# First norm's tables made by TensorE, router logits interleaved with output products, two filler products

## The chip, the cores and the metric

The kernel runs on one core of one Trainium2 chip. The metric is device time in microseconds, from the start to the end of one execution. A core has TensorE (PE in the profile, with its weight loads listed apart as PEld), VectorE (DVE), ScalarE (ACT), GpSimd (POOL) and SyncE (SP, which here issues most of the DMAs), and 16 DMA engines that move data between HBM and the core's SBUF.

## The reference, cut to what matters

384 frames (256 of a new stream, 8 times 16 of running ones) of width 1024 pass one encoder layer. Everything is float32.

```python
m = W_out(concat[beta_ret * Retention(x), beta_conv * ShortConv(x)])   # the mixer
h = LayerNorm1(alpha * x + m)              # gain ln1_g, offset ln1_b
logits = h @ w_router + b_router           # 32 experts, top 4 of 32, softmax over the 4
gate, up = h[tok] @ w_gu[e] + b_gu[e]      # w_gu: 32 x 1024 x 2048, 8 MB an expert
f += g * (((clip(up) + 1) * min(gate) * sigmoid(1.702 * gate)) @ w_down[e] + b_down[e])   # 4 MB an expert
y = LayerNorm2(alpha * h + f)
```

## The kernel before

The program has two parts. The **mixer** projects the input, runs retention and convolution, and multiplies by `w_out`. The **expert part** takes the experts two at a time (a pair), all 32 in turn, and then up to 24 overflow blocks for experts with more than 64 tokens. Each pair needs 24 pieces of weights of 1 MB (128 x 2048 floats): 8 of `w_gu` for each expert, 4 of `w_down` for each expert.

**Rooms.** Pieces land in SBUF in 12 rooms of `ring` and, once the mixer's data are dead, in 4 or 5 of `old_rooms`. Pair 0 uses six side rooms too: `EARLY` (pieces 6 and 7, in `early_rooms`) and `LATE` (pieces 16 to 19, in `over_q`, the last old room, `in_lnp` and `in_xy`). `in_lnp` is the tile `lnp`, 2 x 1024 floats on each partition. Every DMA of weights is issued by SP in the order of the program. SP issues one when the semaphore `piece_used`, which TensorE counts up as it finishes each piece, says that the room is free. So a wait at the head of SP's program holds every transfer behind it.

**Between the mixer and pair 0.** TensorE runs, in program order: the output products (`wout(t, c)`, three float32r products of 512 columns for each of 8 chunks; `t` is one of three tiles of 128 frames, and this is the second half of the output columns), the transposes of the unnormalized rows (`transpose_h(t, n)`, half a row each), the router products (`logits(t, n)`, 32 columns), the ranks of tokens within experts (`early_ranks`, `ranks`), the first products of pair 0's accumulation with the biases (`gate_up_bias(0)`), and the gather of pair 0's tokens (`gather_first`, products with the one-hot `onehot`). VectorE adds the residual and takes row statistics (`residual(t, n)`, which raises `h_raw`; `row_stats`), then picks experts (`choose(t)`, which raises `mask_ready`). In VectorE's program `residual(2, 1)` and `row_stats(2, 3)` stand between `choose(0)` and `choose(1)`. ScalarE copies the transposes and normalizes rows.

**The first norm's gain and offset** are applied to `hid` for all later pairs by VectorE in `gain_and_offset`: three multiplications and three additions of 1024 columns, with both vectors lying in `lnp`, spread over all partitions by two DMAs that ScalarE's queue issues at the end of the mixer. Only after that (`h_ready`) may SP load piece 18 (`LATE[2]`) into `in_lnp`. Pair 0 itself takes gain and offset by column from the small table `ln1_t`. `pair(None)` is pair 0 on TensorE: `gate_up(0)`, `gates`, `count`, `gate_up(1)`, `down(0)`, `down(1)`, and then `gather()` for pair 1.

**Early in the mixer** the semaphore `o_free` tells TensorE that VectorE has read the retention's banks; VectorE raises it before `gate_rows(0)`.

Of the kernel before, what the change touches and what calls it, by code (L numbers as in the profile page):

```python
# [29 lines left out]
ALU = mybir.AluOpType  # L30
# [99 lines left out]
def build(nc, x_tok, x_t, s_ret, conv_in, w_in, w_out, chan, beta_ret, ln1, ln2, w_router, b_router,  # L130
# [3 lines left out]
    with es:  # L134
# [143 lines left out]
        chan_in, bias_in, ln1_in, ln2_in, router_in = map(sem, ("chan_in", "bias_in", "ln1_in", "ln2_in", "router_in"))  # L278
# [13 lines left out]
        gn_var, gn_rstd, o_free, o_ready_m = map(sem, ("gn_var", "gn_rstd", "o_free", "o_ready_m"))  # L292
# [7 lines left out]
        row_shift, norm_ready, h_ready = map(sem, ("row_shift", "norm_ready", "h_ready"))  # L300
        half_gathered, first_xg, first_xg_v = map(sem, ("half_gathered", "first_xg", "first_xg_v"))
# [111 lines left out]
        def _(sp):  # L413
# [87 lines left out]
            def aside_pieces(pair, ea, eb):  # L501
# [6 lines left out]
                for j, units in cycled[:ahead] + aside + cycled[ahead:]:  # L508
# [16 lines left out]
                    if pair == 1 and j == 0:  # L525
                        sp.wait_ge(h_ready, NT)
                        first_side(LATE[2])
# [55 lines left out]
            first_side(LATE[3])  # L583
            sp.wait_ge(logit_mm, NT)
# [32 lines left out]
        def _(pe):  # L617
# [125 lines left out]
            def first_streams():  # L743

                pe.wait_ge(vm_ready, 2)
                pe.wait_ge(o_free, NT)
                pe.wait_ge(stp_out, 1)
                streams(0)
                streams(1)
# [124 lines left out]
            for t in range(NT - 1):  # L874
                wout(t, range(4, KC))
            transpose_h(0, 0)
            transpose_h(0, 1)
            wout(NT - 1, (4,))
            logits(0, 0)
            wout(NT - 1, (5,))  # L880
            logits(0, 1)
            transpose_h(1, 0)
            wout(NT - 1, (6,))
            transpose_h(1, 1)
            wout(NT - 1, (7,))
            logits(1, 0)
            transpose_h(2, 0)
# [15 lines left out]


# [176 lines left out]
            def pair(turn, odd=False, last=False):  # L1081
# [14 lines left out]
                if not first:  # L1096
# [4 lines left out]
                        | ({2: count_before, 6: by_expert} if first else {}))  # L1101
# [3 lines left out]
                     | ({2: overflow_tables} if first else {}) | ({6: lambda: sums_so_far(2)} if last else {}))  # L1105
# [35 lines left out]
        def _(act):  # L1141
# [271 lines left out]
        def _(dve):  # L1413
# [106 lines left out]
            for t in range(NT):  # L1520
# [4 lines left out]
                ins.then_inc(o_free, 1)  # L1525
# [418 lines left out]
```

## Time and profile before

| | |
|---|---|
| median of 3 runs (lowest, highest) | 1113.93 us (1113.84, 1114.98) |
| the profiled execution's own time | 1113.32 us |
| its span, first to last instruction | 1111.4 us |
| TensorE busy | 1073.5 us, 97% |
| VectorE, ScalarE, GpSimd busy | 328.0, 207.4, 90.2 us |
| DMA: bytes, mean rate | 436.27 MB, 393 GB/s |
| mean granted TensorE clock | 0.994 of 2.4 GHz |

The chip's profiler recorded one execution. Busy shares are means over parts with different limits. A TensorE that the profile calls busy may still wait between products, since the ends of matmuls are modelled. A float32 matmul appears as two records. A read of the rate of DMA over short stretches tells when all rooms are full and the transfers stand still.

### The profile page before, as it was taken

What the parts mean: (1) busy time and instruction counts of PE and PEld (TensorE: products, weight loads), DVE (VectorE), ACT (ScalarE), POOL (GpSimd) and SP (SyncE); (2) the same over time, 40 slices, a digit from 0 to 9 for tenths busy, and PEclk for the clock granted to TensorE, in tenths of its full rate; (3) what the DMA queues carried; (4) which work ended last, traced back from release to release, by engine and by line L of the source; (5) the groups of instructions that cost most, each with busy time, mean ns of one, the idle gap of its engine ahead of it and who ended that gap; (6) DMA issues with size and microseconds to landing.
All of it is one profiled execution on the core that took longest, in us unless ns stands there. A gap on an engine that the chain in (4) does not pass through costs nothing.

```text
span 1111.4 us, 13640 instructions
## 1 busy us (share of the span) xinstructions
PE 1073.5 (97%) x5552; PEld 544.8 (49%) x5552; DVE 328.0 (30%) x601; ACT 207.4 (19%) x361; POOL 90.2 (8%) x50
## 2 busy tenths in 40 slices
PE   9999999999999999999999999999898989898995
PEld 6889988344434343434343434343434343342532
DVE  3487764512131312121212121212131312112134
ACT  3243333120111120202020202020111111110122
POOL 4675500000000000000000000000000000000002
PEclk9999999999999999999999999999999999999998
DMA  9972589999999999999999999999999999999995
GB/s 351 325 243 76 163 331 404 364 428 407 426 429 425 428 428 428 426 424 430 429 428 429 427 429 428 429 427 428 430 428 427 429 428 428 426 430 428 428 427 204
DMA packets 56611, 436.27 MB, mean 393 GB/s; under 512 B 8128, under 2 KB 18112, under 8 KB 29088
## 3 DMA queue, kind: packets, MB, share of 16 engines
q1 hardware_dynamic: 50048, 428.68, 92.9%
q10 hardware_dynamic: 6528, 7.09, 1.9%
q8 instruction: 26, 0.43, 0.2%
q14 instruction: 9, 0.07, 0.0%
HBM read 431.78 MB, written 3.97 MB: 392 GB/s over the span
## 4 chain that ended last, share of the span: by engine, by line
PE 67%; DMA 25%; DVE 1%; issue 0%; POOL 0%; ACT 0%; POOLq 0%; SPq 0%; DVEq 0%
PE bank L1012 25%; DMA ring<-w_down 25%; PE bank L1044 18%; PE bank L944 8%; PE bank L637 5%; PE bank L1073 1%; PE bank L993 1%; PE bank L864 1%; PE bank L1075 1%; PE bank L854 1%; PE bank L1021 1%; PE bank L800 1%; PE bank L780 1%; PE bank L786 1%; PE bank L803 1%; PE bank L804 1%
## 5 line engine op out<-in xcount | busy, mean ns | idle before, releaser
L1012 PE MATMUL bank<-ring,xg 128*64 128x512 f32 x1536 | 345.3, 595 | 7.2 <-DMA ring<-w_gu 7.1
L1012 PEld LDWEIGHTS bank<-ring,xg 128*64 128x64 f32 x1536 | 105.0, 136 | 209.1 <-issue 188.0
L1044 PE MATMUL bank<-ring,act_t 128*64 128x512 f32 x672 | 151.0, 595 | 8.3 <-DMA ring<-w_down 8.3
L1012 PE MATMUL bank<-old_rooms,xg 128*64 128x512 f32 x496 | 112.3, 595 | 3.7 <-DMA old_rooms<-w_gu 3.7
L1784 DVE SCALAR_TENSOR_TENSOR oo_lo<-oo_raw,gate_s,oo_hi 128x512 fp32r<-128x512 f32 x32 | 24.0, 752 | 311.0 <-ACT oo_hi L1288 311.0
L1820 DVE TENSOR_SCALAR gate_c<-bank 128x512 f32<-128x512 f32 x32 | 22.1, 691 | 249.8 <-PE bank L1012 249.8
L944 PEld LDWEIGHTS bank<-onehot,hid 128*128 128x128 f32 x720 | 85.9, 196 | 12.2 <-issue 12.2
L1044 PEld LDWEIGHTS bank<-ring,act_t 128*64 128x64 f32 x672 | 46.1, 137 | 92.8 <-issue 78.0
L944 PE MATMUL bank<-onehot,hid 128*128 128x128 f32 x720 | 88.8, 283 | 0.0
L1798 DVE TENSOR_TENSOR xy<-xy,bank 128x512 f32<-128x512 f32 x84 | 52.7, 683 | 107.6 <-PE bank L1075 107.6
L1380 POOL TENSOR_TENSOR rstd<-veps,minus_half 128x1 f32<-128x1 f32 x6 | 3.3, 545 | 961.7 <-DVE veps L1580 961.4
L1363 POOL TENSOR_TENSOR w_parts<-ring,w_parts 128x1024 fp32r<-128x1024 f32 x27 | 74.5, 2764 | 52.8 <-ACT w_parts L1159 52.8
L1012 PEld LDWEIGHTS bank<-old_rooms,xg 128*64 128x64 f32 x496 | 34.2, 136 | 66.7 <-issue 57.6
L1315 ACT COPY oo_raw<-bank 64x512 f32<-64x512 f32 x63 | 36.6, 581 | 159.9 <-PE bank L1044 159.1
L1044 PE MATMUL bank<-old_rooms,act_t 128*64 128x512 f32 x256 | 60.0, 609 | 3.8 <-DMA old_rooms<-w_down 3.8
L1299 ACT ACTIVATE sig<-gate_c 128x512 f32<-128x512 f32 x32 | 20.2, 630 | 177.6 <-DVE gate_c L1820 177.6
L1301 ACT COPY act_t<-bank 128x512 f32<-128x512 f32 x32 | 18.8, 586 | 167.0 <-PE bank L993 167.0
L1277 ACT CAST gt<-bank 128x384 fp32r<-128x384 f32 x16 | 7.7, 479 | 201.2 <-PE bank L956 201.2
L637 PE MATMUL bank<-w_parts,x_hi 128*128 128x512 f32 x180 | 44.8, 395 | 0.3 <-ACT w_parts L1159 0.3
L1159 ACT CAST w_parts<-ring 128x1024 fp32r<-128x1024 f32 x27 | 28.4, 1053 | 65.9 <-PE bank L637 60.3
L1073 PE MATMUL bank<-oo_hi,gt 128*128 128x512 f32 x90 | 38.6, 429 | 0.0
L637 PEld LDWEIGHTS bank<-w_parts,x_hi 128*128 128x128 f32 x180 | 33.6, 187 | 9.5 <-issue 1.5
(258 smaller groups left out, 942.9 us busy)
## 6 DMA issues: line engine op xcount, KB each, us to landing
ring<-w_gu SPq DMA_DIRECT2D x90, 2048.0 KB, 30.0
ring<-w_down SPq DMA_DIRECT2D x41, 2048.0 KB, 33.0
old_rooms<-w_gu SPq DMA_DIRECT2D x30, 2048.0 KB, 28.6
old_rooms<-w_down SPq DMA_DIRECT2D x18, 1024.0 KB, 24.8
old_rooms<-w_down SPq DMA_DIRECT2D x7, 2048.0 KB, 30.5
ring<-w_in SPq DMA_DIRECT2D x13, 1024.0 KB, 14.5
ring<-w_gu SPq DMA_DIRECT2D x12, 1024.0 KB, 6.9
over_q<-w_down SPq DMA_DIRECT2D x3, 2048.0 KB, 15.2
```

The lines of the kernel that those rows point to most:

```text
L637: mm = pe.matmul(out, lhs, rhs, start=(n == 0 and c == 0), stop=(n == 2 and c == KC - 1))
L944: mm = pe.matmul(bank[6 + c // 4][:, (c % 4) * 128:(c % 4 + 1) * 128], hid[:, t, :].rearrange("p (q m k) -> p q k m", m=128, k=GU_RUN) [:, ...
L1012: mm = pe.matmul(bank[2 * a + n][64 * hf:64 * hf + 64, :], xg[:, c, 64 * a:64 * a + 64], w[:, col:col + 512], start=False, stop=(c == KC - 1))
L1044: mm = pe.matmul(bank[b][64 * hf:64 * hf + 64, :], act_t[:, a, c % 4, 64 * (c // 4):64 * (c // 4) + 64], w[:, c % run, hf * 512:(hf + 1) * ...
L1073: pe.matmul(bank[comb_banks[i]][:, :], gt[:, t * 128:(t + 1) * 128], oo_hi[:, hf, :], start=True, stop=False)
L1159: act.copy(w_parts[:, n % PARTS, 0, :], w).then_inc(w_hi_ready, 1)
L1299: act.activation(sig[:, :], gate_c[:, :], ACT.Sigmoid, scale=SIG).then_inc(sig_ready, 1)
L1315: act.copy(oo_raw[64 * a:64 * a + 64, hf, :], bank[down_banks[a]][64 * hf:64 * hf + 64, :]).then_inc(out_ready, 1)
L1363: pool.tensor_tensor(w_parts[:, n % PARTS, 1, :], w, w_parts[:, n % PARTS, 0, :].bitcast(F32), ALU.subtract).then_inc(w_lo_ready, 1)
L1784: dve.scalar_tensor_tensor(oo_lo[:, hf, :], oo_raw[:, hf, :], gate_s[:, 0:1], oo_hi[:, hf, :].bitcast(F32), ALU.mult, ALU.subtract).then_i ...
L1798: dve.tensor_tensor(xy[:, t, o], xy[:, t, o], bank[comb_banks[i]][:, :], ALU.add)\
L1820: dve.tensor_scalar(gate_c[:, :], bank[2 * a][:, :], LIMIT, None, ALU.min).then_inc(gate_ready, 1)
```

## The change

1. `lnp` is no longer loaded by DMA for the first norm. TensorE makes gain and offset over all partitions by itself: `ln1_rows(n)`, eight products of a broadcast column of `ln1_t` with the identity (128 columns each), into banks 0 and 1. It does so twice within pair 0: in `gate_up(1)` ahead of chunk 1, and in `down(0)` ahead of chunk 6. VectorE multiplies or adds straight from the banks (`rows_with`).
2. `LATE[2]` needs no wait on `h_ready` now and is issued right after `LATE[3]`, ahead of `EARLY`.
3. The router's products and transposes are spread between output products of tiles 1 and 2; `gate_up_bias(0)` goes behind the last `logits`.
4. Two products of the identity with constants whose output nobody reads, `keep_busy(384)` and `keep_busy(256)`, stand around `logits(2, 0)` and `early_ranks()`.
5. `o_free` is gone; TensorE waits for `o_ready_m`, raised after `gate_rows(0)`.

```diff
@@ SP
-                    if pair == 1 and j == 0:
-                        sp.wait_ge(h_ready, NT)
-                        first_side(LATE[2])
             sp.wait_ge(h_raw, 2 * NT)
             first_side(LATE[3])
+            first_side(LATE[2])
             sp.wait_ge(logit_mm, NT)
@@ PE
             def first_streams():
                 pe.wait_ge(vm_ready, 2)
-                pe.wait_ge(o_free, NT)
+                pe.wait_ge(o_ready_m, 1)
...
+            def keep_busy(columns):
+                pe.matmul(bank[0][:, 0:columns], ident, cst[:, 0:columns], start=True, stop=True)
+            wout(0, range(4, KC))
             transpose_h(0, 0)
+            wout(1, (4, 5))
             transpose_h(0, 1)
-            wout(NT - 1, (4,))
+            wout(1, (6,))
             logits(0, 0)
-            wout(NT - 1, (5,))
+            wout(1, (7,))
             logits(0, 1)
+            wout(2, (4,))
             transpose_h(1, 0)
-            wout(NT - 1, (6,))
+            wout(2, (5,))
             transpose_h(1, 1)
-            wout(NT - 1, (7,))
+            wout(2, (6,))
             logits(1, 0)
+            wout(2, (7,))
+            logits(1, 1)
             transpose_h(2, 0)
-            logits(1, 1)
             transpose_h(2, 1)
+            keep_busy(384)
             logits(2, 0)
+            early_ranks()
+            keep_busy(256)
+            logits(2, 1)
             pe.wait_ge(sel_ready, 1)
             gate_up_bias(0)
-            early_ranks()
-            logits(2, 1)
...
+            def ln1_rows(n):
+                if n == 0:
+                    pe.wait_ge(up_ready, 1)
+                else:
+                    pe.wait_ge(ln1_used, NT)
+                for c in range(KC):
+                    mm = pe.matmul(bank[c // 4][:, (c % 4) * 128:(c % 4 + 1) * 128],
+                                   ln1_t[:, n, c:c + 1].to_broadcast([128, 128]), ident, start=True, stop=True)
+                mm.then_inc(ln1_mm, 1)
...
-                        | ({2: count_before, 6: by_expert} if first else {}))
+                        | ({1: lambda: ln1_rows(0), 2: count_before, 6: by_expert} if first else {}))
...
-                     | ({2: overflow_tables} if first else {}) | ...
+                     | ({2: overflow_tables, 6: lambda: ln1_rows(1)} if first else {}) | ...
@@ ACT
-            act.wait_ge(piece_used, IN_PIECES + 2)
-            for n in range(2):
-                act.dma_start(lnp[:, n, :], ln1[n:n + 1, :].to_broadcast([128, D])).then_inc(ln1_in, 16)
@@ DVE
-                ins.then_inc(o_free, 1)
+            link(ins)
...
-            def gain_and_offset():
-                dve.wait_ge(ln1_in, 32)
-                for t in range(NT):
-                    ins = dve.tensor_tensor(hid[:, t, :], hid[:, t, :], lnp[:, 0, :], ALU.mult)
-                link(ins)
-                for t in range(NT):
-                    dve.tensor_tensor(hid[:, t, :], hid[:, t, :], lnp[:, 1, :], ALU.add).then_inc(h_ready, 1)
+            def rows_with(n, op, done):
+                dve.wait_ge(ln1_mm, n + 1)
+                for t in range(NT):
+                    dve.tensor_tensor(hid[:, t, :].rearrange("p (b n) -> p b n", b=2),
+                                      hid[:, t, :].rearrange("p (b n) -> p b n", b=2), banks[:, 0:2, :], op)\
+                        .then_inc(done, 1)
...
-            gain_and_offset()
...
                             slots_of(p + 1)
+                        if first:
+                            rows_with(0, ALU.mult, ln1_used)
...
                 if first:
                     tables()
+                    dve.wait_ge(ln1_used, NT)
+                    rows_with(1, ALU.add, h_ready)
```

How TensorE's order moves. First, the end of the router: before, from the last output product's follower to the gather (L814 are transposes, L827 logits, L864 the bias products, L840 and L841 ranks, L854 the gather):

```order
L804 MATMUL bank<-out_parts,mixed_lo 128x512
L827 MATMUL bank<-gg,xt 128x32 x4
L814 MATMUL bank<-cst,hid 128x128 x4
L827 MATMUL bank<-gg,xt 128x32 x4
L814 MATMUL bank<-cst,hid 128x128 x4
L827 MATMUL bank<-gg,xt 128x32 x4
L864 MATMUL bank<-biasp,sel 64x512 x4
L841 MATMUL bank<-vv,cst 128x32
L840 MATMUL bank<-vv 128x32
L841 MATMUL bank<-vv,cst 128x32
L827 MATMUL bank<-gg,xt 128x32 x4
L854 MATMUL bank<-onehot,hid 128x128 x13
```

The same place after the change, where every line number is one less and L875 is `keep_busy`, from the last record of `wout(2, 7)` on:

```order
L803 MATMUL bank<-out_parts,mixed_lo 128x512
L826 MATMUL bank<-gg,xt 128x32 x4
L813 MATMUL bank<-cst,hid 128x128 x8
L875 MATMUL bank<-cst 128x384
L826 MATMUL bank<-gg,xt 128x32 x4
L840 MATMUL bank<-vv,cst 128x32
L839 MATMUL bank<-vv 128x32
L840 MATMUL bank<-vv,cst 128x32
L875 MATMUL bank<-cst 128x256
L826 MATMUL bank<-gg,xt 128x32 x4
L863 MATMUL bank<-biasp,sel 64x512 x4
L853 MATMUL bank<-onehot,hid 128x128 x13
```

The bias products went from ahead of the ranks to the end, two fillers came in, and all output products now stand ahead of `logits(1, 1)`.

Second, TensorE in pair 0's second `gate_up`, from the bias products to the transposes of the activations (L1012 are products of `gate_up`, L913 and L914 `count_before`), before:

```order
L864 MATMUL bank<-biasp,sel 64x512 x4
L1012 MATMUL bank<-ring,xg 64x512 x8
L913 MATMUL bank<-vv,cst 96x1
L914 MATMUL bank<-vv 1x1
L1012 MATMUL bank<-ring,xg 64x512 x8
L993 MATMUL bank<-cst,act_h 128x128 x4
```

and after, where L1030 are the products of `gate_up` and L919 is `ln1_rows`:

```order
L863 MATMUL bank<-biasp,sel 64x512 x4
L1030 MATMUL bank<-ring,xg 64x512 x4
L919 MATMUL bank<-cst,ln_t 128x128 x8
L1030 MATMUL bank<-ring,xg 64x512 x4
L931 MATMUL bank<-vv,cst 96x1
L932 MATMUL bank<-vv 1x1
L1030 MATMUL bank<-ring,xg 64x512 x8
```

Eight products came in behind chunk 0, that is ahead of the room-freeing piece 9 and all that follow; eight more stand in `down(0)` ahead of chunk 6.

Third, SP's issues between the mixer and pair 1's weights, before (`xy` is `LATE[3]`, `lnp` is `LATE[2]`, L490 are pieces of pair 1):

```order
L479 DMA ring<-w_gu 128x2048 x7
L483 DMA xy<-w_down 128x2048
L479 DMA early_rooms<-w_gu 128x2048 x2
L483 DMA ring<-w_down 128x2048 x2
L490 DMA ring<-w_gu 128x4096
L483 DMA lnp<-w_down 128x2048
L490 DMA ring<-w_gu 128x4096 x4
```

and after:

```order
L480 DMA ring<-w_gu 128x2048 x7
L484 DMA xy<-w_down 128x2048
L484 DMA lnp<-w_down 128x2048
L480 DMA early_rooms<-w_gu 128x2048 x2
L484 DMA ring<-w_down 128x2048 x2
L491 DMA ring<-w_gu 128x4096 x5
```

`LATE[2]` moved from behind the first piece of pair 1 to the place ahead of `EARLY`.

## Rows read from the trace of the kernel before

**Rows 1.** The page: its span line and the rate in 40 equal slices.

```profile
span 1111.4 us, 13640 instructions
GB/s 351 325 243 76 163 331 404 364 428 407 426 429 425 428 428 428 426 424 430 429 428 429 427 429 428 429 427 428 430 428 427 429 428 428 426 430 428 428 427 204
```

**Rows 2.** Stretches: sum, PE, PEld, DVE, ACT, POOL busy, granted clock, DMA share, GB/s.

```profile
196.00:198.00 2.00, 2.00 (x12) 0.67 (x10) 2.00 (x3) 0.00 (x0) 0.00 (x0) 1.00 0.44 90
...
254.00:258.00 4.00, 4.00 (x21) 1.15 (x17) 0.00 (x0) 0.00 (x0) 0.00 (x0) 1.00 0.88 299
302.00:1092.00 790.00, 766.92 (x3900) 329.10 (x3898) 162.63 (x280) 114.73 (x212) 0.00 (x0) 1.00 1.01 427
```

**Rows 3.** Timeline of SP's DMA issues: start, duration, line, tile.

```profile
195.97 0.33 SPq L483 DMA_DIRECT2D ring<-w_down  x1
...
202.50 0.33 SPq L483 DMA_DIRECT2D lnp<-w_down  x1
...
244.81 0.33 SPq L490 DMA_DIRECT2D ring<-w_gu  x1
...
254.66 0.33 SPq L494 DMA_DIRECT2D ring<-w_down  x1
```

**Rows 4.** The chain that ended last: start, duration, piece.

```profile
251.18 6.87 PE bank L1012 x32
...
305.73 6.87 PE bank L1012 x32
...
640.13 31.91 DMA ring<-w_down
```

**Rows 5.** Timeline of TensorE from the last output product to pair 0.

```profile
179.84 0.39 PE L804 MATMUL bank<-out_parts,mixed_lo 128*128 128x512 f32 x1
...
182.63 0.98 PE L827 MATMUL bank<-gg,xt 128*128 128x32 f32 x8
...
184.38 0.41 PE L841 MATMUL bank<-vv,cst 128*128 128x32 f32 x2 [0.22 <-DVE vv L1649]
...
186.19 4.55 PE L854 MATMUL bank<-onehot,hid 128*128 128x128 f32 x26
...
191.16 2.90 PE L854 MATMUL bank<-onehot,hid 128*128 128x128 f32 x22
193.99 10.52 PE L1012 MATMUL bank<-ring,xg 128*64 128x512 f32 x48
```

**Rows 6.** Timeline of VectorE around the choice of tile 1's experts.

```profile
180.34 0.69 DVE L1598 SCALAR_TENSOR_TENSOR hid<-xy,bank 128x512 f32<-128x512 f32 x1 [0.31 <-PE bank L804]
...
182.36 0.25 DVE L1639 SCALAR_TENSOR_TENSOR vv<-bank,rstd,vv 128x32 f32<-128x32 f32 x1 [0.17 <-PE bank L827]
...
183.95 0.37 DVE L1649 TENSOR_REDUCE vv<-vv 128x32 f32<-128x128 f32 x1
```

**Rows 7.** Stretches of 2 us in which the granted clock fell.

```profile
186.00:188.00 2.00, 2.00 (x10) 2.00 (x11) 1.48 (x10) 1.97 (x5) 0.00 (x0) 0.50 1.03 434
188.00:190.00 2.00, 2.00 (x15) 2.00 (x14) 0.37 (x1) 0.30 (x2) 0.00 (x0) 0.72 1.03 426
...
230.00:232.00 2.00, 2.00 (x6) 0.57 (x8) 0.45 (x3) 0.00 (x0) 0.00 (x0) 0.52 1.00 426
232.00:234.00 2.00, 2.00 (x8) 0.56 (x4) 0.00 (x0) 0.00 (x0) 0.00 (x0) 0.62 1.03 442
```

**Rows 8.** Timeline of TensorE: raw float32 products, the gather for pair 1.

```profile
4.77 5.42 PE L669 MATMUL bank<-ring,hid 128*128 128x512 f32 x12
...
244.70 5.92 PE L944 MATMUL bank<-onehot,hid 128*128 128x128 f32 x48
```

**Rows 9.** Timelines of VectorE and TensorE where `o_free` is waited for.

```profile
115.79 2.22 DVE L1530 TENSOR_TENSOR qo<-qo,gg 128x512 f32<-128x512 f32 x1
117.99 1.15 PE L739 MATMUL bank<-tmp,kk 32*128 32x256 f32 x16
```

**Rows 10.** The page's costliest groups: VectorE's sums from a bank.

```profile
L1798 DVE TENSOR_TENSOR xy<-xy,bank 128x512 f32<-128x512 f32 x84 | 52.7, 683 | 107.6 <-PE bank L1075 107.6
```

More of the change, by code:

```diff
@@ L277, in build @@
         xt_in, x_in, cst_in, mcst_in, st_in = map(sem, ("xt_in", "x_in", "cst_in", "mcst_in", "st_in"))
-        chan_in, bias_in, ln1_in, ln2_in, router_in = map(sem, ("chan_in", "bias_in", "ln1_in", "ln2_in", "router_in"))
+        chan_in, bias_in, ln2_in, router_in = map(sem, ("chan_in", "bias_in", "ln2_in", "router_in"))
         rows_stored, retp_stored = sem("rows_stored"), sem("retp_stored")
@@ L291, in build @@
         chan_mm, c_out, u_out, conv_ready = map(sem, ("chan_mm", "c_out", "u_out", "conv_ready"))
-        gn_var, gn_rstd, o_free, o_ready_m = map(sem, ("gn_var", "gn_rstd", "o_free", "o_ready_m"))
+        gn_var, gn_rstd, o_ready_m = map(sem, ("gn_var", "gn_rstd", "o_ready_m"))
         kd_ready, stp_mm, stp_out = sem("kd_ready"), sem("stp_mm"), sem("stp_out")
@@ L300, in build @@
         row_shift, norm_ready, h_ready = map(sem, ("row_shift", "norm_ready", "h_ready"))
+        ln1_mm, ln1_used = sem("ln1_mm"), sem("ln1_used")
         half_gathered, first_xg, first_xg_v = map(sem, ("half_gathered", "first_xg", "first_xg_v"))
@@ L873, in _ @@
             router_sums()
-            for t in range(NT - 1):
-                wout(t, range(4, KC))
+            def keep_busy(columns):
+                pe.matmul(bank[0][:, 0:columns], ident, cst[:, 0:columns], start=True, stop=True)
+            wout(0, range(4, KC))
             transpose_h(0, 0)
+            wout(1, (4, 5))
             transpose_h(0, 1)
-            wout(NT - 1, (4,))
+            wout(1, (6,))
             logits(0, 0)
-            wout(NT - 1, (5,))
+            wout(1, (7,))
             logits(0, 1)
+            wout(2, (4,))
             transpose_h(1, 0)
-            wout(NT - 1, (6,))
+            wout(2, (5,))
             transpose_h(1, 1)
-            wout(NT - 1, (7,))
+            wout(2, (6,))
             logits(1, 0)
+            wout(2, (7,))
+            logits(1, 1)
             transpose_h(2, 0)
-            logits(1, 1)
             transpose_h(2, 1)
+            keep_busy(384)
             logits(2, 0)
+            early_ranks()
+            keep_busy(256)
+            logits(2, 1)
             pe.wait_ge(sel_ready, 1)
             gate_up_bias(0)
-            early_ranks()
-            logits(2, 1)
             pe.wait_ge(first_slots, 1)
@@ L1104, in pair @@
                 down(0, turn, odd, {4: lambda: transpose_act(1, p, 2 if first else DN_RUN)}
-                     | ({2: overflow_tables} if first else {}) | ({6: lambda: sums_so_far(2)} if last else {}))
+                     | ({2: overflow_tables, 6: lambda: ln1_rows(1)} if first else {}) | ({6: lambda: sums_so_far(2)} if last else {}))
                 if not first and not last:
@@ L1524, in _ @@
                                             gmv[:, t, h, 0:1], grs[:, t, h:h + 1], ALU.subtract, ALU.mult)
-                ins.then_inc(o_free, 1)
+            link(ins)
             def gate_rows(t):
-                dve.wait_ge(o_free, t + 1)
                 dve.tensor_tensor(qo[:, t, :], qo[:, t, :], gg[:, t, :], ALU.mult).then_inc(o_ready_m, 1)
```

## The prediction

> **What bounds the kernel now.** I read the page's rates by slice first. From the sixth slice of 27.8 us on, the DMA engines move 404 to 430 GB/s nearly everywhere [rows 1], and over the 790 us from 302 us to 1092 us they average 427 [rows 2]. The total is the time at which this stream of weights runs without a break, plus the bytes still to come divided by that rate. A piece of 1 MB (1.049 million bytes) takes 1.049/0.427 = 2.46 us. What counts is therefore the last place where the stream stands still.
>
> The stretches show two such places after the mixer. Near 196 us the rate is only 90 GB/s [rows 2]: all rooms are full, and the first is given back by pair 0, whose products start at 193.99 us [rows 5]; SP issues the refill at 195.97 us [rows 3]. The second is the one that matters: over the 4 us from 254 us the rate is 299 GB/s, a loss of (427-299)/427 x 4 = 1.2 us [rows 2]. SP's timeline says why. It issues a run at 244.81 us and then nothing until 254.66 us [rows 3]. No room comes free in between, since TensorE does the gather for pair 1 (from 244.70 us, 5.92 us [rows 8]) and then has to finish two chunks of pair 1, whose products start near 251.18 us [rows 4]. The DMAs had finished all that they had. **At 254.66 us the stream thus waits for TensorE, not TensorE for it.** After that it never stands still again: TensorE does a pair in 305.73-251.18 = 54.55 us [rows 4], while 24 pieces take 24 x 2.46 = 59.0 us to load, so TensorE eats into its lead by 4.5 us a pair until, at 640.13 us, the chain of waits passes to the DMA [rows 4].
>
> From this follows how to price the change. Up to about 254 us any DMA saved or moved only lengthens the second gap. The end moves by as much as TensorE's start of pair 1 moves. From there on the instructions of both kernels are the same.
>
> **The change part by part.**
>
> **Fewer and earlier DMAs: 0.** Two loads for the norm (together 1 MB written) go, and `LATE[2]` is loaded into the gap at 194 to 198 us, where before it was issued at 202.50 us [rows 3]. Each is worth one piece, 2.46 us, to the DMA, but the stream then merely arrives 2.46 us earlier at the wait that ends with the issue of 254.66 us. If TensorE started pair 1 earlier, the DMA's head start would be needed; 1.2 us of earlier start could be used even without it.
>
> **`o_free` to `o_ready_m`: +0.2.** TensorE's `streams` start at 117.99 us, and `gate_rows(0)` takes VectorE until 115.79+2.22 = 118.01 us [rows 9]. The new wait ends about there, plus a `link` and a semaphore, so 0 to 0.3. Behind it in TensorE's queue stand the products of the mixer, on which everything waits.
>
> **The new order around the logits, at full clock: +0.7.** Before, `wout(2, 7)` ends about 0.23 us after its last record starts: 180.07 us [rows 5], and VectorE's `residual(2, 1)` starts at 180.34 [rows 6]. Now one more `logits` (the spacing from 182.63 to the next instruction is about 0.8 [rows 5]) plus two changes of kind of product at 0.1 stand ahead of it: 181.1. `residual(2, 1)` then starts at 181.35. VectorE used to go through residual and statistics and reach `choose(1)` at 182.36, having waited 0.17 for the logits [rows 6]; now it gets there at 181.35 + (182.36-0.17-180.34) = 183.2, and nothing is waited for. `choose(1)` takes 183.95+0.37-182.36 = 1.96 us [rows 6], so the mask is there at 185.2 instead of 184.3.
>
> TensorE meanwhile needs from 181.1: `logits(1, 1)` 0.8, two transposes 0.8, the filler, `logits(2, 0)` 0.8. A raw float32 product of 512 columns takes two records of 5.42/12 = 0.45 us [rows 8], so 384 columns cost 2 x 0.34 = 0.68, and 256 columns 0.45. TensorE arrives at the ranks at 184.2 and **waits 1.0 us for the mask**, where before it waited 0.22 [rows 5] after the bias products had covered the rest. Then come ranks 0.7, filler 0.5, logits 0.8, bias 0.5 and 0.1 to 0.2 for changes of kind: the gather starts at 187.9, against 186.19 [rows 5]. At full clock, 22 records of the gather took 193.99-191.16 = 2.83 us [rows 5], 0.129 each; 48 take 6.2, plus 0.6 for the last ranks. Pair 0 starts at 187.9+6.8 = 194.7 instead of 193.99: +0.7. This already includes the 1.1 us of fillers.
>
> **The clock: in the +0.7 or not.** The granted clock fell to its lower level (1.2 GHz) after a stretch of narrow products: 0.50 from 186 us and 0.72 from 188 us [rows 7]. The first 26 records of the gather show 4.55 us [rows 5]; less 0.17 for the last record's tail that is 4.4, where 26 x 0.129 = 3.4 would do. So it cost 1.0 us there, and about 0.3 on the last logits. The fillers and wide products may keep it up; I take that they do. If not, pair 0 starts 1.4 us later. The second fall, 0.52 and 0.62 from 230 us [rows 7], costs (0.48+0.38) x 2 = 1.7 us of TensorE. The 24-column products of the overflow tables ahead of it stay where they are, and I leave it as it is; should it go, that is 1.7 us gained.
>
> **`ln1_rows`, twice: +4.1.** Eight raw float32 products of 128 columns with 128 x 128 weights each, in two records: 32 records. The nearest row has the same shape, the gather with 48 records from 244.70 to about 250.55, 0.122 each [rows 8]. So 32 x 0.122 = 3.9, plus 0.2 to 0.3 for changing the kind of product four times. A broadcast column as the weights is not in the trace; below, 32 records at the 0.1 us of the narrow ones [rows 5] give 3.2, above, 32 x 0.17 as in the slowed gather [rows 5] give 5.4. I take 4.1. TensorE has practically no idle time in pair 0 that could take this in, and both calls stand ahead of room-freeing pieces.
>
> **VectorE's six passes: 0.** From a bank 512 columns take 0.683 us [rows 10], so three tiles take 3 x 1.37 = 4.1 us. The first three start after `slots_of(1)` and are over well before `gate_up(1)` ends, when VectorE is next needed. The last three can start some 9 us ahead of the gather that waits for `h_ready` (two chunks of `down(0)` and all of `down(1)`), so 4.9 us are spare. Were the `tables` ahead of them 5 us late, the gather would wait.
>
> **Sum.** 0.2 + 0.7 + 4.1 = +5.0 us on the profiled execution's 1113.32: **1118.3 us**. The runs' median before was 0.6 higher than that execution; I leave that in the range.
>
> **Rivals.**
>
> *The stream's own account (faster).* One piece less after the gap near 196 us and no wait on `h_ready` save 2.46 us: 1113.3-2.5 = 1110.9. It would hold if the DMAs were busy without a break from 198 us on. The rate of 299 GB/s at 254 us [rows 2] speaks against it: there they wait for a room. It decides only if TensorE starts pair 1 no later than before, and it is to start 5 us later. 7 in 100.
>
> *The fillers don't hold the clock.* The wait of 1.0 us, the 32-column products and the transposes stay dense behind the last output product, and a filler of 0.68 us is small beside them. Then +6.4, and 1119.7. The fall after the 24-column products, with no wait beside them, speaks for it; that the clock stayed up while output products lay between the logits speaks against. 28 in 100. The Trainium skill (TensorE: Matmul & The Clock Gate, Part 4) says that transposes do not count as a busy TensorE in the same way, which speaks for this rival and would give its 1119.7; the trace cannot tell transposes from the narrow products around them.
>
> *Both falls go, and the mask's wait is shorter than worked out.* Then 5.0-1.7-0.8 = +2.5, or 1115.8; with `ln1_rows` at its lower bound of 3.2 it is +1.6, 1114.9, which is not to be told from no change. 18 in 100, half of it within the bound.
>
> *The forecast:* 45 in 100, with its own range of 1117 to 1119.3. The remaining 2 are for something else.
>
> **Numbers.** A measurement of this kernel can tell about 0.2%, 2.2 us, from no change. Slower: the forecast, the lost clock and half of the third rival, 82 in 100. The same: 11. Faster: 7. The range leaves out the faster case: from 1115.0 (third rival near its lower end) to 1120.5 (lost clock, half of the offset to the median and dearer `ln1_rows`).
>
> **What would show each step.** In the profile after: the rate near 196 us is high and the gap before pair 1's third run of weights is longer than before, about 1.2 + 2.5 us or more, and SP's issue that stood at 254.66 stands near 259.7; TensorE's gather for pair 1 starts near 249.7; VectorE's row for the mask of tile 1 ends near 185.2 and a wait of about 1 us stands at the ranks; pair 0 starts near 194.7; `ln1_rows` shows twice 16 records in 2 us; the granted clock near 186 us tells which of two cases it is. I would be wrong if the stream stood still again later than pair 1, if broadcast weights were loaded much faster or slower, or if the stream were not waiting for a room at 254 us.

## The result, and the profile after

| | before | after |
|---|---|---|
| median of 6 runs (lowest, highest) | 1114.95 us (1113.84, 1115.63) | 1119.46 us (1118.27, 1119.89) |
| ratio, 95% interval | | 1.0044 [1.0034, 1.0055], +4.9 us [3.8, 6.1] |
| the profiled execution (its span) | 1113.32 us (1111.4) | 1119.89 us (1117.9) |

The change made the kernel slower by 0.44%, and 1118.3 us had been forecast: +5.0 us, added to the profiled execution's 1113.32 us, which lies 1.6 us below the median of before that stands beside this result. The profiled executions differ by more than the medians do, by 6.6 us; 1.5 us of that are one slow step near the end, which the change does not always bring (below, at the table of **P**). The page of the profile after, its span and the rate in 40 slices, answers to [rows 1]: the same steady 425 to 430 GB/s, now ending later.

```profile
span 1117.9 us, 13710 instructions
GB/s 352 326 235 81 157 343 356 353 416 373 426 429 427 430 425 428 427 426 429 429 428 429 426 429 429 427 429 428 427 430 426 429 430 427 427 429 426 429 428 176
```

The stretches of the profile after (sum, PE, PEld, DVE, ACT and POOL busy, granted clock, DMA share, GB/s), against [rows 2, 7]:

```profile
186.00:188.00 2.00, 2.00 (x16) 1.50 (x16) 1.16 (x5) 1.98 (x3) 0.00 (x0) 1.00 1.02 430
196.00:198.00 2.00, 2.00 (x12) 0.72 (x10) 1.72 (x11) 0.00 (x0) 0.00 (x0) 1.00 1.05 393
232.00:234.00 2.00, 2.00 (x10) 0.77 (x11) 0.45 (x3) 0.00 (x0) 0.00 (x0) 0.72 0.98 418
234.00:236.00 2.00, 2.00 (x7) 0.66 (x4) 0.00 (x0) 0.00 (x0) 0.00 (x0) 0.50 1.05 451
256.00:258.00 2.00, 2.00 (x12) 0.62 (x10) 0.00 (x0) 0.00 (x0) 0.00 (x0) 1.00 0.67 287
258.00:263.00 5.00, 5.00 (x24) 1.75 (x21) 0.00 (x0) 0.00 (x0) 0.00 (x0) 1.00 0.59 177
302.00:1097.00 795.00, 769.94 (x3915) 330.36 (x3916) 162.57 (x280) 115.31 (x213) 0.00 (x0) 1.00 1.00 427
```

The change did what it says for the DMAs: at 196 us they are busy (393 GB/s, before 90). The price shows at 256 to 263 us: (427-287)/427 x 2 + (427-177)/427 x 5 = 3.6 us of the stream are lost there, before 1.2. What was saved early has become idle time in front of the same wait.

SP's issues, against [rows 3]:

```profile
182.67 0.71 SPq L484 DMA_DIRECT2D lnp<-w_down  x1
...
196.27 0.33 SPq L484 DMA_DIRECT2D ring<-w_down  x1
...
249.29 0.33 SPq L491 DMA_DIRECT2D ring<-w_gu  x1
259.13 0.33 SPq L495 DMA_DIRECT2D ring<-w_down  x1
```

`LATE[2]` is issued 20 us earlier (182.67 us, before 202.50), and the run of weights at pair 1's third chunk 4.47 us later (259.13, before 254.66).

TensorE's timeline, against [rows 5, 8, 9]: the early wait, the ranks, the gather, pair 0's start, the two `ln1_rows`, the gather for pair 1.

```profile
118.14 1.15 PE L738 MATMUL bank<-tmp,kk 32*128 32x256 f32 x16
...
185.20 0.41 PE L840 MATMUL bank<-vv,cst 128*128 128x32 f32 x2 [0.71 <-DVE vv L1662]
...
187.86 3.17 PE L853 MATMUL bank<-onehot,hid 128*128 128x128 f32 x26
...
194.29 10.52 PE L1030 MATMUL bank<-ring,xg 128*64 128x512 f32 x48
...
211.68 2.05 PE L919 MATMUL bank<-cst,ln_t 128*128 128x128 f32 x16
213.66 1.94 PE L1030 MATMUL bank<-ring,xg 128*64 128x512 f32 x8
...
238.25 2.05 PE L919 MATMUL bank<-cst,ln_t 128*128 128x128 f32 x16
240.23 1.94 PE L1062 MATMUL bank<-xy,act_t 128*64 128x512 f32 x8
...
249.18 5.92 PE L962 MATMUL bank<-onehot,hid 128*128 128x128 f32 x48
```

Pair 0 starts 0.30 us later, with the clock at 1.00 in this gather, where in the profile before it fell; from there to the gather for pair 1 TensorE needs 249.18-194.29 = 54.89 us, before 244.70-193.99 = 50.71: 4.18 us more, of which the two calls take 1.98 us each (213.66-211.68 and 240.23-238.25).

VectorE's mask of tile 1 and the last three passes, against [rows 6]:

```profile
184.77 0.38 DVE L1662 TENSOR_REDUCE vv<-vv 128x32 f32<-128x128 f32 x1
...
240.43 3.48 DVE L1643 TENSOR_TENSOR hid<-hid,bank 128x1024 f32<-128x1024 f32 x3 [7.60 <-PE bank L919]
```

The mask is there at 185.15 us, and TensorE waits 0.71 us for it. The passes end at 243.9 us, 5.3 us ahead of the gather.

### The profile page after: what moved, and what is told of

It reads as the page before. It is cut to its first block, busy times and chain, and to the rows that moved or that the text cites. A ratio compares the mean times of both kernels' runs of the same rounds, so it can differ in the third digit from the quotient of the medians.

```text
span 1117.9 us, 13710 instructions
## 1 busy us (share of the span) xinstructions
PE 1077.4 (96%) x5588; PEld 547.7 (49%) x5588; DVE 328.0 (29%) x601; ACT 207.6 (19%) x361; POOL 90.2 (8%) x50
## 4 chain that ended last, share of the span: by engine, by line
PE 67%; DMA 25%; DVE 1%; issue 0%; POOL 0%; ACT 0%; POOLq 0%; SPq 0%; DVEq 0%
PE bank L1030 25%; DMA ring<-w_down 25%; PE bank L1062 18%; PE bank L962 8%; PE bank L636 5%; PE bank L1091 1%; PE bank L1011 1%; PE bank L863 1%; PE bank L1093 1%; PE bank L1039 1%; PE bank L799 1%; PE bank L853 1%; PE bank L779 1%; PE bank L785 1%; PE bank L803 0%; PE bank L802 0%
## 5 line engine op out<-in xcount | busy, mean ns | idle before, releaser
L1030 PE MATMUL bank<-ring,xg 128*64 128x512 f32 x1536 | 345.5, 595 | 8.9 <-DMA ring<-w_gu 8.5
L1030 PEld LDWEIGHTS bank<-ring,xg 128*64 128x64 f32 x1536 | 105.0, 136 | 210.3 <-issue 187.0
L1030 PE MATMUL bank<-old_rooms,xg 128*64 128x512 f32 x496 | 112.3, 595 | 3.7 <-DMA old_rooms<-w_gu 3.7
L1030 PEld LDWEIGHTS bank<-old_rooms,xg 128*64 128x64 f32 x496 | 34.2, 136 | 66.7 <-issue 57.3
```

The source lines that it names most:

```text
L1030: mm = pe.matmul(bank[2 * a + n][64 * hf:64 * hf + 64, :], xg[:, c, 64 * a:64 * a + 64], w[:, col:col + 512], start=False, stop=(c == KC - 1))
```

## The experiments

All times are medians of device time beside runs of the kernel before on the same chip. The ratio is formed from all the runs and not from the two medians, so it can differ from their quotient; the differences in us and their intervals are those of the ratio, times 1114 us. A single kernel's runs spread over 3 to 5 us here, so the trace of each is read too. **P** is the time at which SP issues the third run of pair 1's weights, the issue of 254.66 us in [rows 3].

**The norm's tables alone.** The kernel after with the old order around the logits and no fillers:

```diff
 # after, with the sequence from wout(0, ...) to logits(2, 1) as in before
-            keep_busy(384)
...
-            keep_busy(256)
```

> The kernel after with the old order of TensorE around the logits and without the two fillers, so only the norm's tables, LATE[2]'s place and o_ready_m are changed. My theory (TensorE's start of pair 1 sets the end): the two calls of ln1_rows cost 4.2 us, the wait for gate_rows 0.15, so +4.3 us on the kernel before, and the gather for pair 1 starts 4.3 us later than 244.7. The account by the stream of weights: one piece is loaded in the gap near 196 us, so -2.5 us.

Measured: 1117.47 us beside 1114.77, ratio 1.0027 [1.0015, 1.0040], +3.0 us [1.7, 4.5]. P is 257.39. The sign and the size rule out the stream's account (-2.5); 4.3 is within the interval, at its upper end. The gather for pair 1 starts at 247.43 us, 2.7 us later than before and not 4.3. The reason is a surprise in this trace: without any filler, the clock did not fall near 186 us, and pair 0 starts at 192.60 us, 1.4 us earlier than before.

```profile
186.18 3.17 PE L853 MATMUL bank<-onehot,hid 128*128 128x128 f32 x26
```

```profile
186.00:188.00 2.00, 2.00 (x18) 1.93 (x18) 1.73 (x11) 1.97 (x4) 0.00 (x0) 1.00 1.00 422
```

**The order and the fillers alone.** The kernel before with the whole new sequence:

```diff
-            for t in range(NT - 1):
-                wout(t, range(4, KC))
...
+            wout(0, range(4, KC))
+            transpose_h(0, 0)
+            wout(1, (4, 5))
...
+            keep_busy(384)
+            logits(2, 0)
+            early_ranks()
+            keep_busy(256)
+            logits(2, 1)
+            pe.wait_ge(sel_ready, 1)
+            gate_up_bias(0)
```

> The kernel before with the new order around the logits and the two fillers, nothing else. My theory: pair 0 starts within 0.3 us of before (1.1 us of fillers and 0.7 us of a longer wait for the mask against 1.3 us of lost clock), so within 0.5 us of the kernel before. If the fillers and the wait were the main cost of the whole change: +1.8 us or more. If the clock were the main gain: -1 us or more.

Measured: 1116.81 us beside 1114.77, ratio 1.0017 [1.0005, 1.0028], +1.9 us [0.6, 3.1]. P is 256.74, +2.08 on before, whose profile has the same two falls of the clock; pair 0 starts at 196.11 us, 2.12 us later. I had expected it within 0.3 us and the time within 0.5, so this missed, and the account that makes the order a main cost (+1.8 or more) came true. With the fillers in place the clock fell all the same: the first 26 records of the gather took 4.70 us, not 3.17.

```profile
188.16 4.70 PE L854 MATMUL bank<-onehot,hid 128*128 128x128 f32 x26
```

```profile
188.00:190.00 2.00, 2.00 (x10) 1.84 (x9) 1.51 (x9) 1.18 (x4) 0.00 (x0) 0.50 0.98 410
190.00:192.00 2.00, 2.00 (x14) 2.00 (x13) 0.00 (x0) 0.00 (x0) 0.00 (x0) 0.65 1.03 397
```

So this part is a loss of its own. The two parts add up to the whole, 3.0 + 1.9 = 4.9 us; each of them is known to 1.2 to 1.5 us only.

**`LATE[2]` back at its place.** The kernel after, with this load issued behind the first piece of pair 1 again:

```diff
             first_side(LATE[3])
-            first_side(LATE[2])
...
+                    if pair == 1 and j == 0:
+                        first_side(LATE[2])
```

> The kernel after with LATE[2] issued at its old place, behind the first piece of pair 1 (without the wait on h_ready). My theory: within 0.3 us of the kernel after, +4.5 us on before, since the stream waits for a room at about 259 us either way. The account by the stream: the load goes back from an idle gap into busy time, 2.5 us slower than after, +7 us on before.

Measured: 1119.81 us beside 1114.77, ratio 1.0046 [1.0032, 1.0060], +5.1 us [3.6, 6.7]. P is 259.37. Near 196 us the stream stands nearly still again (16 GB/s), and the end does not care, since the gap around P takes it in (229 GB/s over 258 to 262 us, 287 and 177 in the profile after):

```profile
258.00:262.00 4.00, 4.00 (x22) 1.28 (x20) 0.00 (x0) 0.00 (x0) 0.00 (x0) 1.00 0.74 229
196.00:198.00 2.00, 2.00 (x12) 0.77 (x12) 1.66 (x7) 0.87 (x3) 0.00 (x0) 1.00 0.04 16
```

**One useless piece more.** The kernel after, with piece 6 loaded twice:

```diff
             for j in EARLY:
                 first_side(j)
+            sp.wait_ge(side_full[EARLY[0]], 16)
+            first_side(EARLY[0])
...
-                    pe.wait_ge(side_full[j], 16)
+                    pe.wait_ge(side_full[j], 32 if j == EARLY[0] else 16)
```

> The kernel after with one useless load more: piece 6 is loaded a second time, ahead of pair 0's first refill (1 MB, 2.46 us of the stream; TensorE waits for both). My theory: the gap of about 3.6 us at 256 to 262 us takes it in; within 0.3 us of the kernel after, +4.5 us on before, and the gap is 2.5 us shorter. The account by the stream: 2.5 us slower than after, +7 us on before.

Measured: 1118.91 us beside 1114.77, ratio 1.0038 [1.0025, 1.0052], +4.2 us [2.8, 5.8]: as after, not 2.5 more. P is 259.71. The gap around the third run did get shorter, by less than I had written (2.5):

```profile
258.00:262.00 4.00, 4.00 (x20) 1.26 (x18) 0.00 (x0) 0.00 (x0) 0.00 (x0) 1.00 0.69 213
256.00:264.00 8.00, 8.00 (x40) 2.94 (x35) 0.20 (x1) 0.30 (x1) 0.00 (x0) 1.00 0.81 305
```

Over the 8 us from 256 us, (427-305)/427 x 8 = 2.3 us are lost; in the profile after, the same 8 us have 244 GB/s, 3.4 us. That is 1.1 us less, with P 0.6 us later. The stream's account of the time is wrong by this run and the one before it: its +7 us lies outside both intervals, outside that of c_late2_back only just.

**No fillers.** The kernel after without the two calls:

```diff
-            keep_busy(384)
...
-            keep_busy(256)
```

> The kernel after without its two filler products. Theory that the fillers hold the clock: the fall near 186 us comes in every run, +1.3 us of lost clock against 0.5 us of filler saved, so 0.8 us slower than after, +5.3 us on before. Rival, after the first four runs, whose profiles show that fall with fillers (b, c, d) and without them (a): the fall comes or stays away by chance, and taking the fillers out saves the 0.5 us of the second one (the first only fills the wait for the mask), so 0.5 us faster than after, +4 us on before.

Measured: 1119.93 us beside 1114.25, ratio 1.0055 [1.0039, 1.0071], +6.1 us [4.3, 7.9]. After had +4.9 [3.8, 6.1]; the two intervals overlap, and neither theory is picked out by the times.

```profile
181.24 0.39 PE L803 MATMUL bank<-out_parts,mixed_lo 128*128 128x512 f32 x1
...
185.52 0.41 PE L840 MATMUL bank<-vv,cst 128*128 128x32 f32 x2 [0.79 <-DVE vv L1660]
...
187.75 4.79 PE L853 MATMUL bank<-onehot,hid 128*128 128x128 f32 x26
```

The last output product starts 0.32 us later here than in the profile after (180.92 us), so the stage is best counted from there: to the gather it is 187.75-181.24 = 6.51 us, with fillers 187.86-180.92 = 6.94. Of the fillers only 0.43 us come back: the first lies in the wait for the mask (0.79 us here, 0.71 with it), the second, 0.52 us, behind it. P is 259.08. The clock fell near 188 us, as it had with fillers in b_order_only, c_late2_back and d_extra_piece.

**The bias products back in the wait, one filler.** The kernel before with the new order, but (against b_order_only)

```diff
             keep_busy(384)
             logits(2, 0)
+            pe.wait_ge(sel_ready, 1)
+            gate_up_bias(0)
             early_ranks()
-            keep_busy(256)
             logits(2, 1)
-            pe.wait_ge(sel_ready, 1)
-            gate_up_bias(0)
```

> The kernel before with the new order around the logits, the first filler (384 columns) alone, and the bias products ahead of the ranks as before, where they stand in the wait for the mask. My account: against the order of b_order_only this saves the second filler (0.5 us) and the bias products (0.5 us, now in the wait), so the gather starts 1.1 us earlier than in b (187.9 to 188.2 us there): near 186.9, and the time is about 1 us below b, +0.7 us on before. Rival (order costs nothing, only the clock counts): same as b_order_only, +1.9 us.

Measured: 1113.85 us beside 1114.25, ratio 1.0003 [0.9992, 1.0015], +0.3 us [-0.9, 1.7]. The gather starts at 186.98 us, as worked out (186.9), 1.18 us earlier than in b_order_only, of which 0.16 us are an earlier start of the last output product. The wait for the mask is down to 0.16 us:

```profile
185.27 0.41 PE L841 MATMUL bank<-vv,cst 128*128 128x32 f32 x2 [0.16 <-DVE vv L1656]
```

The clock fell nowhere in this trace, P is 252.47 and the gap in front of pair 1 is closed (434 GB/s over 252 to 256 us):

```profile
230.00:234.00 4.00, 4.00 (x20) 1.47 (x18) 0.00 (x0) 0.59 (x1) 0.00 (x0) 1.00 1.00 430
252.00:256.00 4.00, 4.00 (x19) 1.19 (x16) 0.00 (x0) 0.00 (x0) 0.00 (x0) 1.00 1.03 434
```

**The overflow tables in three parts.** The kernel before, with the narrow products ahead of three chunks of `down(0)` instead of one:

```diff
-            def overflow_tables():
+            def overflow_tables(t):
...
-                     | ({2: overflow_tables} if first else {})
+                     | ({t + 1: lambda t=t: overflow_tables(t) for t in range(NT)} if first else {})
```

> The kernel before with the overflow tables' narrow products in three parts, ahead of chunks 1, 2 and 3 of down(0), instead of all ahead of chunk 2. If the density of narrow products sets the second fall (near 230 us), it goes: TensorE starts pair 1 up to 1.7 us earlier; the stream can use 1.2 us of that, so -1.2 us on before, and its gap near 256 us closes. If it comes anyway: no change.

Measured: 1113.14 us beside 1114.25, ratio 0.9997 [0.9987, 1.0007], -0.3 us [-1.4, 0.8]. In its trace the clock stays at 1.00 from 230 to 234 us, P is 253.48 (1.18 earlier) and the stream runs at 401 GB/s through 253 to 257 us. The time is not to be told from before, and the -1.2 us that I had worked out is not excluded either. One profile without the fall does not show that it never comes; the mean clock over its 12 runs was 0.9956, beside 0.9945 over the 23 of before.

```profile
230.00:234.00 4.00, 4.00 (x24) 2.06 (x24) 0.45 (x3) 0.58 (x1) 0.00 (x0) 1.00 0.98 418
253.00:257.00 4.00, 4.00 (x21) 1.18 (x16) 0.00 (x0) 0.00 (x0) 0.00 (x0) 1.00 1.00 401
```

**3.84 us of TensorE, nothing else, in pair 0.** Kernel before; the output of these products is not read:

```diff
+            def extra_products(p):
+                pe.wait_ge(up_ready, 2 * p + 1)
+                for n in range(16):
+                    pe.matmul(bank[n // 4 % 2][:, (n % 4) * 128:(n % 4 + 1) * 128], ident, ident, start=True, stop=True)
...
                         | ({2: count_before, 6: by_expert} if first else {})
+                        | ({1: lambda: extra_products(p)} if first else {}))
```

> The kernel before with 16 products of the identity with itself (32 records, as many as both calls of ln1_rows have, about 3.9 us of TensorE; their output is not read) in pair 0, ahead of chunk 1 of gate_up(1). No DMA, no VectorE work and no order is changed. My theory: TensorE starts pair 1 3.9 us later, and so does the end: +3.9 us on before. Rival (the stream bounds the kernel throughout and TensorE's extra work hides beneath it): within 0.5 us of before.

Measured: 1116.21 us beside 1114.45, ratio 1.0028 [1.0016, 1.0040], +3.1 us [1.8, 4.5]. The products take 3.84 us, and P is 255.63, though the clock fell at neither place. It costs what `ln1_rows` costs in a_ln1_only (+3.0). That TensorE's time in pair 0 moves the end is shown by this, and the rival (within 0.5 us) is out; the full 3.9 us lie within the interval.

```profile
210.08 3.84 PE L909 MATMUL bank<-cst 128*128 128x128 f32 x32
```

**The same in pair 3.** The same products in the kernel before, but placed there:

```diff
-                        | ({1: lambda: extra_products(p)} if first else {}))
+                        | ({1: lambda: extra_products(p)} if type(turn) is tuple and turn[0] == 3 else {}))
```

> The same 16 products at the same place of pair 3, about 160 us later. My theory: the stream is never short of a room there (TensorE's lead on it has grown by two pairs), so the end does not move: within 0.5 us of before. If TensorE set the time wherever it is busy: +3.9 us, as in pair 0.

Measured: 1115.41 us beside 1114.45, ratio 1.0016 [1.0008, 1.0025], +1.8 us [0.9, 2.8]. Not zero, not 3.9. SP issues nothing between 397.48 and 415.02 us, and a gap appears, where the kernel before moves 430 and 426 GB/s over the same 8 us:

```profile
397.48 0.33 SPq L490 DMA_DIRECT2D ring<-w_gu  x1
415.02 0.33 SPq L490 DMA_DIRECT2D ring<-w_gu  x1
```

```profile
412.00:416.00 4.00, 4.00 (x20) 1.26 (x18) 0.00 (x0) 0.00 (x0) 0.00 (x0) 1.00 0.69 287
416.00:420.00 4.00, 4.00 (x24) 1.38 (x22) 0.10 (x1) 1.49 (x3) 0.00 (x0) 1.00 1.00 356
```

(427-287)/427 x 4 + (427-356)/427 x 4 = 2.0 us. My statement that the stream is never short of a room after 258 us was true of the kernel before, but the margin at this second place is only 3.84-2.0 = 1.8 us, and more work than that comes through.

**Half of it in pair 3.** As g_late_pair3, with 8 products:

```diff
-                for n in range(16):
+                for n in range(8):
```

> As g_late_pair3, with 8 products (1.9 us) instead of 16. In g, SP issued no load for 17.5 us before 415.02 us (in the kernel before, it is 393.47 to 411.01 us), since pair 4 has no side rooms, and a gap of about 2 us stood there. So a second place where the stream nearly waits for TensorE lies at 411 us with 3.8-2.0 = 1.8 to 1.9 us to spare. Theory: 1.9 us of TensorE in pair 3 is just taken in, within 0.4 us of before. Rival (TensorE's time before 640 us counts in proportion): +0.8 us, half of g's.

Measured: 1114.51 us beside 1114.57, ratio 1.0001 [0.9989, 1.0013], +0.1 us [-1.2, 1.4]. In the trace the rate is 320 GB/s over 412 to 416 us, a loss of 1.0 us, so the margin is rather 1 to 1.8 us. The time agrees with a margin; proportion (+0.8) is not excluded by the interval.

**The same 16 products in 11 later pairs.** The kernel before with them, but placed there:

```diff
-                        | ({1: lambda: extra_products(p)} if first else {}))
+                        | ({1: lambda: extra_products(p)} if turn is not None and type(turn) is not tuple and not last else {}))
```

> The same 16 useless products in each of the 11 pairs from the fifth to the last but one, 11 x 3.84 = 42 us of TensorE in all. Theory: from pair 4 on the stream alone sets the pace; TensorE needs 54.6+3.8 = 58.4 us a pair against 59 us of the stream, so the end moves by less than 1 us. Rival (a TensorE that is 97 percent busy bounds the kernel): +20 to +42 us.

Measured: 1128.07 us beside 1114.57, ratio 1.0117 [1.0099, 1.0135], +13.0 us [11.0, 15.0]. Neither number. The chain of waits shows what I overlooked:

```profile
435.19 3.77 PE bank L909 x32
...
493.68 3.77 PE bank L909 x32
...
1103.34 6.89 PE bank L1050 x32
```

TensorE now needs 493.68-435.19 = 58.49 us a pair and never catches up with the stream; the DMAs have little left to do from 1092 us on (20 GB/s over the next 4 us), and TensorE works off its arrears alone. An estimate agrees: in the kernel before, TensorE makes up some 4.5 us a pair and reaches the stream at 640 us, so at the start of the fifth pair (414.89 us) it is (640.13-414.89)/54.55 x 4.5 = 18.6 us behind; from there it makes up 59.0-58.49 = 0.5 us in each of 11 pairs, and 13 us are left at the end. Of 42.2 us, 42.2-13.0 = 29 were taken in. So the end is the later of two: the stream, set by its gaps, and TensorE's own work.

**Fillers in the old order.** Kernel before, with two calls added:

```diff
+            keep_busy(384)
             logits(2, 0)
+            keep_busy(256)
```

> The kernel before, its order kept, with the two fillers around logits(2, 0), ahead of the bias products. If they hold the clock near 186 us: 1.1 us of fillers, of which 0.3 us go into the wait for the mask, against 1.3 us of clock: -0.5 to 0 us, and no run's mean clock at 0.993. If they don't, as the runs so far say: +0.8 us, with the mean clocks spread as those of before.

Measured: 1112.97 us beside 1114.45, ratio 1.0001 [0.9990, 1.0012], +0.1 us [-1.1, 1.3], which excludes neither of the two expectations. Its trace has no fall near 188 us but the one near 230; one of the 12 runs had a mean clock of 0.993, and their mean was 0.9953, beside 0.9943 of before (29 runs). a_ln1_only and h_late_pair0, with no fillers, had 0.9952 and 0.9954, b_order_only, with both, 0.9937. Whether fillers ever hold the clock is thus **open**; that they did not reliably hold it is shown by b_order_only, c_late2_back and d_extra_piece. A form with the second filler ahead of `logits(2, 1)`, as in the kernel after, was planned too and gave no time: in the old order the sum of the bias products is still open there in the bank into which the filler would write.

**P and the span** of the profiled executions whose edits stand ahead of P, with the time at which the granted clock first rose to 2.4 GHz (the first entry of the clock's record in the trace):

| kernel | clock first rose, us | clock fell near 186-190, 230-236 | P, us | span, us | span - P |
|---|---|---|---|---|---|
| before | 4.81 | yes, yes | 254.66 | 1111.4 | 856.7 |
| after | 4.18 | no, yes | 259.13 | 1117.9 | 858.8 |
| a_ln1_only | 6.12 | no, yes | 257.39 | 1115.8 | 858.4 |
| b_order_only | 7.07 | yes, yes | 256.74 | 1115.9 | 859.2 |
| c_late2_back | 7.00 | yes, no | 259.37 | 1117.9 | 858.5 |
| d_extra_piece | 7.29 | yes, no | 259.71 | 1116.4 | 856.7 |
| e_no_fillers | 7.16 | yes, no | 259.08 | 1117.7 | 858.6 |
| f_bias_ahead | 6.85 | no, no | 252.47 | 1110.3 | 857.8 |
| i_spread | 5.59 | yes, no | 253.48 | 1110.9 | 857.4 |
| h_late_pair0 | 6.55 | no, no | 255.63 | 1112.9 | 857.3 |
| k2_fillers | 4.53 | no, yes | 253.86 | 1110.7 | 856.8 |

P ranges over 7.2 us and the remainder over 2.5. Whatever was done ahead of P, the rest takes 858 us with 1.3 us either way. In three of these profiles, part of a long remainder is a single step near the end of the chain that ended last. The last such step of the profile after, and the same step in d_extra_piece, whose order of TensorE is the same:

```profile
1053.87 36.06 DMA ring<-w_down
```

```profile
1053.75 34.72 DMA ring<-w_down
```

The steps of this kind ahead of it take 34.5 to 34.7 us in both. One of 36.1 us stands in b_order_only and in c_late2_back too, and none in before. Why they come is open; d_extra_piece, which has the whole change, has none. The long remainders of a_ln1_only and e_no_fillers have no such step, and their cause is open too.

## Why the prediction came out right, and where it did not

**The stream waits for TensorE at pair 1, so TensorE's start sets the end: right**, by h_late_pair0 (only TensorE's work added), c_late2_back and d_extra_piece (only the stream changed) and the table. The order of size of the gap was right too: 3.6 us lost, about 3.7 forecast.

**Fewer and earlier DMAs, 0: right** (c_late2_back and d_extra_piece).

**`o_ready_m`, +0.2: right**, 118.14 against 117.99 us.

**`ln1_rows`, +4.1: right**, 4.18 us in the trace between pair 0's start and the gather; by the measured times of a_ln1_only, which has `o_ready_m` as well, +3.0 [1.7, 4.5].

**VectorE's passes, 0: right**, 5.3 us spare where 4.9 was worked out.

**The order around the logits, +0.7: the gather's start was right (187.86, forecast 187.9), the step was not.** TensorE waited 0.71 us for the mask, forecast 1.0, and pair 0 started 0.30 us later in the profile after, because the first 26 records of the gather took 3.17 us there, 0.12 each, and not the 0.129 each of the working. The step put the lost clock on one side only, as something that the fillers give back. The profile after looks like that, since its clock did not fall near 186 us. But b_order_only, with both falls as before, costs +2.08 us in P and +1.9 in time, and a_ln1_only kept the clock without a filler. The fall comes in some executions and not in others, with and without fillers. What the order costs at equal clock is 0.7 + 1.4 = 2.1 us by the prediction's own figures (fillers, longer wait, bias products no longer in the wait), and 2.12 us at pair 0's start in b_order_only; f_bias_ahead took 1.0 us of it back.

**Why the sum held nevertheless: in part by luck.** At equal clock the working gives +6.4 us, which is the rival *The fillers don't hold the clock*, and +4.9 [3.8, 6.1] was measured, whose upper end is just below that. So the number that came near was reached with a gain that the fillers did not reliably bring. Some of the difference is in which runs had the clock. Put by their mean clock, the runs of a_ln1_only lie 4.3 us above those of before at 0.994 and below (3 runs beside 18) and 3.9 us at 0.996 and above (4 beside 10); those of b_order_only lie 2.0 us above (9 beside 18) and 1.3 us (2 beside 10). The two parts then sum to 6.3 us where the clock was low and to 5.2 where it was high. These are few runs, sorted afterwards. An explanation of the smaller sum at the high clock was only argued: where the clock does not fall, TensorE of before would be ready at P about 3 us earlier, but the stream could use only the 1.2 us of its gap, while after, whose gap is 3.6 us, can use it all. The traces of f_bias_ahead (P 2.19 us earlier than before, span 1.1 us shorter) and i_spread (1.18 and 0.5) fit this. The times of before itself do not: its runs at 0.996 and above are 2.9 us faster than those at 0.994 and below, not 1.2. That part stays open.

**A clause that failed:** that nothing later matters. At 411 us the stream has only 1 to 1.8 us to spare (g_late_pair3, m_half_pair3). The change shifts TensorE and the stream together, so it should leave that margin as it was; no run tests this by itself.

## What to carry to other kernels

Where a stream of loads is the bound, look for its last gap and for who ends it. A load saved or added ahead of that gap changed nothing here as long as the gap was longer than the load. Work added to the engine that ends the gap cost about its length (3.84 us cost 3.1 [1.8, 4.5]), even though that engine waits for loads in every pair from 640 us on. The room to spare differs from place to place (none in pair 0, 1 to 2 us in pair 3, 29 us over the later pairs), so a saving and its price have to be looked up at the same place. A filler that stands where its engine waits anyway costs nothing; one behind the wait costs its length (0.43 us came back of 0.52 when both were taken out).

## What the hardware showed unexpectedly

The granted clock fell to 1.2 GHz after the same instructions in some profiled executions and not in others (table above), each time over less than 4 us, at two places between its first rise and TensorE's last product: the 26 first records of the gather took 3.17 us without and 4.52 to 4.80 with the fall. Runs of the kernel before had mean clocks of 0.992 to 0.997, and in the 29 runs beside the first four experiments the 6 with 0.997 averaged 1111.7 us, the 13 with 0.993 averaged 1115.2. So 3.5 us of the spread of this kernel's times goes with the clock, and one profile cannot tell what an edit does to it.

The traces hold more than that: **the falls are tied to the moment at which the clock first rose.** That it was low before this moment is told by the first raw products, 12 records: from 4.77 us they took 5.42 us in the profile before [rows 8], whose clock rose at 4.81 us, and 1.1 us more in b_order_only, whose clock rose at 7.07:

```profile
4.79 6.54 PE L669 MATMUL bank<-ring,hid 128*128 128x512 f32 x12
```

In all nine profiles that show the first fall (before, b_order_only, c_late2_back, d_extra_piece, e_no_fillers, i_spread, g_late_pair3, m_half_pair3, n_late_rest) it begins 180.9 us after that moment, though the moment itself lies anywhere from 4.69 to 7.29 us and the instructions that run then are not the same. The second fall begins 225.3 us after it in seven profiles and 228.7 in the profile after. So where in an execution this moment lies decides which instructions a possible fall meets. With the order of the kernel before, the first fall came at 4.69 to 5.59 us (before, g_late_pair3, i_spread, m_half_pair3, n_late_rest) and not at 6.12 and 6.55 us (a_ln1_only, h_late_pair0). Two comparisons at nearly the same moment say more of an edit than the others do: with both fillers (c_late2_back, d_extra_piece; 7.00 and 7.29 us) and without (e_no_fillers, 7.16 us) the first fall came alike; and g_late_pair3 and i_spread, at 5.58 and 5.59 us, differ ahead of 230 us only in the overflow tables, and the second fall came in g_late_pair3 alone. k2_fillers, without the first fall at 4.53 us beside m_half_pair3 with it at 4.69 us, hints that fillers may hold the clock at that moment; it is one pair of profiles, 0.16 us apart.

The Trainium skill (TensorE: Matmul & The Clock Gate, Part 1) says that the clock gate runs on its own time base and that the same kernel varies with its phase. The fixed distances of 180.9 and 225.3 us agree with this.

A stationary operand that is one column repeated 128 times was loaded as fast as any: 16 records in 1.98 us, 0.124 each, beside 0.122 in the gather [rows 8].
